# Attention order of a two-layer head-group mixer: half-width products gathered into three groups per head pair

## The reference, cut to what matters

```python
def block_attention(q, k, v, scale):           # 20 maps: 6 of gqa, 8 of diff, 6 of mla
    s = einsum('bqkgd,blkd->bkgql', q, k) * scale
    p = softmax(s, axis=-1)
    return einsum('bkgql,blkd->bqkgd', p, v)
# latent queries read context and latent keys (256 + 512); context queries read context keys only
o_a  = block_attention(ql_a, [kc_a, kl_a], [vc_a, vl_a], 64**-0.5)
o_b  = diff_out(block_attention(q1l, ...), block_attention(q2l, ...), lam, ...)   # o1 - lam*o2, rms norm
o_m  = block_attention(ql_m, [kc_m, kl_m], [vc_m, vl_m], 96**-0.5)
if ctx_out:                                     # layer 0 only
    oc_a, oc_b, oc_m = the same with context queries, context keys and values
h = concat([o_a * silu(g_a), o_b * silu(g_b), o_m * silu(g_c)])
y = h @ w_out
```

## Time and profile before

| | |
|---|---|
| runs before | 1100.06, 1102.35, 1105.29 us |
| the profiled execution | 1105.77 us, its span 1103.9 us |
| TensorE busy | 969.0 us (88%) |
| VectorE, ScalarE, GpSimd busy | 594.0, 403.4, 524.8 us |
| mean granted TensorE clock | 0.928 of full speed |
| TensorE's share of the chain that ended last | 71% |

### The profile page before, as it was taken

The page is one execution under the profiler, slowest core; times in us unless marked ns, Lnnn a source line. Parts: engine busy times, 40 slices in busy tenths (PEclk is TensorE's granted clock), DMA queues, the critical chain, the costliest instruction groups (busy, mean ns, idle before and its releaser), DMA issues.

```text
span 1103.9 us, 13093 instructions
## 1 busy us (share of the span) xinstructions
PE 969.0 (88%) x4607; PEld 684.6 (62%) x4607; DVE 594.0 (54%) x901; ACT 403.4 (37%) x815; POOL 524.8 (48%) x421
## 2 busy tenths in 40 slices
PE   4799999996899899998995299899968999999793
PEld 2478777985554455555784289789755445555572
DVE  5419230244568499824069548341645758782337
ACT  1521122314354466554200333133434445555320
POOL 2227232352557455553345337243626756566464
PEclk9799999996899899999998689899959989899997
DMA  9756451215232100012431022123142130001421
GB/s 364 270 178 218 157 188 40 77 31 125 55 77 65 34 16 8 16 58 79 169 96 77 38 62 72 58 65 85 49 101 65 37 72 16 15 16 58 160 69 77
DMA packets 44976, 96.91 MB, mean 88 GB/s; under 512 B 9592, under 2 KB 16656, under 8 KB 42864
## 3 DMA queue, kind: packets, MB, share of 16 engines
q1 hardware_dynamic: 43472, 90.83, 26.8%
q10 hardware_dynamic: 1440, 5.24, 1.2%
HBM read 71.33 MB, written 5.26 MB: 69 GB/s over the span
## 4 chain that ended last, share of the span: by engine, by line
PE 71%; DVE 10%; POOL 4%; ACT 4%; SPq 4%; DMA 3%; issue 3%; POOLq 0%; ACTq 0%; DVEq 0%
PE banks L762 13%; PE banks L764 12%; PE banks L763 12%; PE banks L936 11%; PE banks L956 9%; PE banks L914 5%; SPq L588 3%; PE banks L773 2%; DMA area_g<-in_w_ada_dram 2%; DVE negmax L1635 1%; PE banks L975 1%; DVE stats L1515 1%; DVE area_b L1779 1%; PE banks L968 1%; PE banks L826 1%
## 5 line engine op out<-in xcount | busy, mean ns | idle before, releaser
L1393 POOL TENSOR_TENSOR w_split<-w_raw,w_split 128x512 fp32r<-128x512 f32 (+4 forms) x124 | 146.2, 1184 | 258.7 <-ACT w_split L1138 258.6
L762 PE MATMUL banks<-w_split,area_a 128*128 128x512 f32 (+3 forms) x624 | 232.7, 373 | 16.4 <-DVE area_a L1845 9.9
L764 PE MATMUL banks<-w_split,area_a 128*128 128x512 f32 (+3 forms) x624 | 229.8, 368 | 0.0
L763 PE MATMUL banks<-w_split,area_a 128*128 128x512 f32 (+3 forms) x624 | 229.7, 368 | 0.0
L1635 DVE TENSOR_REDUCE negmax<-banks 128x1 f32<-128x768 f32 x160 | 149.6, 951 | 67.3 <-PE banks L914 66.4
L1138 ACT ACTIVATE w_split<-w_raw 128x512 fp32r<-128x512 f32 (+4 forms) x124 | 69.9, 581 | 278.1 <-PE banks L764 278.1
L936 PE MATMUL banks<-area_a 97*128 97x512 f32 (+4 forms) x448 | 135.7, 416 | 17.5 <-DMA area_a<-m_row 11.5
L762 PEld LDWEIGHTS banks<-w_split,area_a 128*128 128x128 f32 x624 | 119.4, 191 | 46.2 <-issue 16.4
L1237 ACT ACTIVATE area_z<-banks 128x512 f32<-128x512 f32 x196 | 109.1, 595 | 103.5 <-PE banks L936 98.2
L764 PEld LDWEIGHTS banks<-w_split,area_a 128*128 128x128 f32 x624 | 118.9, 190 | 16.6
L763 PEld LDWEIGHTS banks<-w_split,area_a 128*128 128x128 f32 x624 | 119.2, 191 | 15.5
(11 more groups left out here) (184 smaller groups left out, 1458.4 us busy)
## 6 DMA issues: line engine op xcount, KB each, us to landing
area_g<-in_w_ada_dram SPq DMA_DIRECT2D x16, 1024.0 KB, 5.8
w_raw<-in_w_in_dram SPq DMA_DIRECT2D x32, 512.0 KB, 3.7
area_g<-in_w_ada_dram SPq DMA_DIRECT2D x16, 512.0 KB, 5.0
w_raw<-in_w_out_dram SPq DMA_DIRECT2D x16, 512.0 KB, 3.9
area_a<-parts SPq DMA_DIRECT2D x72, 96.0 KB
area_a<-parts SPq DMA_DIRECT2D x30, 192.0 KB, 3.6
area_b<-in_x_dram SPq DMA_DIRECT2D x8, 512.0 KB, 9.8
x_mid<-area_b ACTq DMA_DIRECT2D x6, 512.0 KB, 2.7
```

Source lines behind the costliest of these rows:

```text
L762: nc.tensor.matmul(dst, a[0], b[0], start=first, stop=False)
L763: nc.tensor.matmul(dst, a[0], b[1], start=False, stop=False)
L764: return nc.tensor.matmul(dst, a[1], b[0], start=False, stop=last)
L1393: op = nc.gpsimd.tensor_tensor(lo, raw, hi.bitcast(F32), ALU.subtract)
```

## The change

Each `attend(L)` is rewritten around one loop over p = 0 to 10, in which pair p is scored while pair p-1 is finished:

- In layer 0 the context scores of a pair come first instead of last.
- The half-width products stand in three groups per step: `mix(p-1, 4)` and `mix(p-1, 5)`; then the context product, `mix(p, 0)`, `mix(p, 1)` and `denominators`; then `mix(p, 2)` and `mix(p, 3)`. The context denominators of pair p and the latent ones of pair p-1 share one call, so there is one more call (p = 0) in layer 0.
- How many maximum tiles stand between them is read from the table `max_counts`.
- `turn_max(p+1)` comes earlier in a step (except at p = 0).
- On ScalarE `mla_high(2p+6)` now follows the last exponent and `squares` at the end of step p; `mla_high(2p+5)` stands between the exponents of steps 2 and 3.
- On GpSimd the gate of pair p-1 comes before the fourth sum, block 10 is split after that sum, and a diff pair's gate comes a step later.
- The rows of ones of all diff units and of four mla units are written once per layer: eight transfers in a row after the maxima of pair 1 (`load_ones`). Units 12 and 13 are loaded in turn 4 instead of 3, unit 14 in 4 instead of 5, unit 16 in 5 instead of 6.
- Reciprocals are a step of their own; the copied context output has two buffers.

The diff, cut to this:

```diff
+def max_counts(L, p):
+
+    if L < DEPTH - 1:
+        return {0: [1, 2, 0, 1, 2, 1, 1, 1, 0, 1, 3], 1: [1, 1, 2, 2, 1, 1, 0, 1, 1, 1, 0]}.get(p, [1, 1, 1, 1, 1, 1, 0, 1, 1, 1, 0])
+    return {0: [1, 0, 1, 1, 2, 1, 1, 0, 1, 1, 2], 1: [2, 1, 1, 1, 1, 1, 0, 1, 1, 1, 0]}.get(p, [1, 0, 1, 1, 1, 1, 0, 1, 1, 1, 0])
+
+
 NRING = 3
...
-            def load_one(row, done):
-                move(row.rearrange("o (t n) -> o t n", n=P), across(ones_r[:], TILES)).then_inc(done, 16)
+            def load_ones():
+
+                for b in range(1, 2 * KD, 2):
+                    move(blocks[96:97, b, :].rearrange("o (t n) -> o t n", n=P), across(ones_r[:], TILES)).then_inc(ones_in, 16)
 
...
-                    for u in {-1: (2, 3), 0: (4, 5), 1: (6, 7), 2: (8, 9), 3: (10, 11, 12, 13), 5: (14, 15),
-                              6: (16, 17), 7: (18, 19)}.get(p, ()):
+                    for u in {-1: (2, 3), 0: (4, 5), 1: (6, 7), 2: (8, 9), 3: (10, 11), 4: (12, 13, 14), 5: (15, 16),
+                              6: (17,), 7: (18, 19)}.get(p, ()):
                         load_unit(L, u)
...
                 if L == 0:
                     pe.wait_ge(ada_ready, 2)
-                for i in range(len(max_tiles(L))):
-                    max_tile(L, 0, i)
+                tiles = iter([(p, i) for p in range(NPAIR) for i in range(len(max_tiles(L)))])
+
+                def maxima(n):
+                    for p, i in itertools.islice(tiles, n):
+                        max_tile(L, p, i)
+
+                maxima(len(max_tiles(L)))
                 turn_max(L, 0)
...
-                for p in range(1, NPAIR):
-                    scores(L, p, 0)
-                    max_tile(L, p + 1, 6)
-                    scores(L, p, 1)
-                    max_tile(L, p + 1, 7)
-                    if context:
-                        mix(L, p - 1, "ctx")
-                    else:
+                for p in range(NPAIR + 1):
+                    c = max_counts(L, p)
+                    now = p < NPAIR
+                    if now and context:
+                        scores(L, p, "ctx")
+                    maxima(c[0])
+                    if now:
+                        scores(L, p, 0)
+                    maxima(c[1])
+                    if p:
                         mix(L, p - 1, 4)
                         mix(L, p - 1, 5)
-                    scores(L, p, 2)
-                    max_tile(L, p + 1, 8)
-                    denominators(L, p - 1)
-                    scores(L, p, 3)
-                    max_tile(L, p + 2, 0)
-                    turn_denominators(L, p - 1)
-                    turn_output(L, p - 1)
-                    mix(L, p, 0)
-                    max_tile(L, p + 2, 1)
-                    turn_max(L, p + 1)
-                    mix(L, p, 1)
+                    maxima(c[2])
+                    if now:
+                        scores(L, p, 1)
+                    maxima(c[3])
+                    if now:
+                        if context:
+                            mix(L, p, "ctx")
+                        mix(L, p, 0)
+                        mix(L, p, 1)
+                    if p or context:
+                        denominators(L, p)
+                    if p:
+                        turn_max(L, p + 1)
+                    maxima(c[4])
+                    if now:
+                        scores(L, p, 2)
+                    maxima(c[5])
+                    if now:
+                        scores(L, p, 3)
+                    maxima(c[6])
                     if head_pair(p + 3):
                         mla_head(L, 2 * p + 6)
-                    scores(L, p, 4)
-                    max_tile(L, p + 2, 2)
-                    scores(L, p, 5)
-                    max_tile(L, p + 2, 3)
-                    mix(L, p, 2)
-                    max_tile(L, p + 2, 4)
+                    if now:
+                        mix(L, p, 2)
+                        mix(L, p, 3)
+                    if p or context:
+                        turn_denominators(L, p)
+                    maxima(c[7])
+                    if p:
+                        turn_output(L, p - 1)
+                    maxima(c[8])
+                    if now:
+                        scores(L, p, 4)
+                    maxima(c[9])
+                    if p == 0:
+                        turn_max(L, 1)
                     if head_pair(p + 3):
                         mla_head(L, 2 * p + 7)
-                    mix(L, p, 3)
-                    max_tile(L, p + 2, 5)
-                    if context:
-                        scores(L, p, "ctx")
-                        mix(L, p, 4)
-                        mix(L, p, 5)
-
-                if context:
-                    mix(L, NPAIR - 1, "ctx")
-                else:
-                    mix(L, NPAIR - 1, 4)
-                    mix(L, NPAIR - 1, 5)
-                denominators(L, NPAIR - 1)
-                turn_denominators(L, NPAIR - 1)
-                turn_output(L, NPAIR - 1)
+                    if now:
+                        scores(L, p, 5)
+                    maxima(c[10])
 
...
@@ -1285,50 +1293,47 @@
                 split_block(L, 2)
                 copy_maxrow(L, 0)
 
-                exponent(L, 0, 0)
-                exponent(L, 0, 1)
-                split_block(L, 4)
-                for s in range(2, 6):
-                    exponent(L, 0, s)
-                copy_maxrow(L, 1)
-                split_block(L, 6)
-                if context:
-                    exponent(L, 0, "ctx")
-
-                for p in range(1, NPAIR):
-                    exponent(L, p, 0)
-                    if context:
+                for p in range(NPAIR + 1):
+                    now = p < NPAIR
+                    if now and context:
+                        exponent(L, p, "ctx")
+                    if now:
+                        exponent(L, p, 0)
+                    if p:
                         copy_latents(L, p - 1)
-                    if head_pair(p + 2):
-                        mla_high(L, 2 * p + 4)
-                    exponent(L, p, 1)
-                    if context:
-                        copy_context(L, p - 1)
-                    else:
-                        copy_latents(L, p - 1)
+                    if now:
+                        exponent(L, p, 1)
+                    if p == 0:
+                        split_block(L, 4)
+                    if now and context:
+                        copy_context(L, p)
+                    if p or context:
+                        copy_denominators(L, p)
+                    if p:
+                        copy_maxrow(L, p + 1)
+                    if now:
+                        exponent(L, p, 2)
                     if head_pair(p + 2):
                         mla_high(L, 2 * p + 5)
-                    exponent(L, p, 2)
-                    copy_denominators(L, p - 1)
-                    exponent(L, p, 3)
-                    copy_maxrow(L, p + 1)
+                    if now:
+                        exponent(L, p, 3)
                     if head_pair(p + 3):
                         mla_copy(L, 2 * p + 6)
-                    exponent(L, p, 4)
-                    exponent(L, p, 5)
+                    if now:
+                        exponent(L, p, 4)
+                    if p == 0:
+                        copy_maxrow(L, 1)
+                        split_block(L, 6)
+                    if head_pair(p + 3):
+                        mla_copy(L, 2 * p + 7)
+                    if now:
+                        exponent(L, p, 5)
                     if (L, p - 1) in N_NORMED:
                         squares(L, p - 1)
-                    if head_pair(p + 3):
-                        mla_copy(L, 2 * p + 7)
                     if p == 2:
                         split_block(L, 10)
-                    if context:
-                        exponent(L, p, "ctx")
-
-                copy_latents(L, NPAIR - 1)
-                if context:
-                    copy_context(L, NPAIR - 1)
-                copy_denominators(L, NPAIR - 1)
+                    if head_pair(p + 3):
+                        mla_high(L, 2 * p + 6)
 
...
@@ -1464,27 +1469,24 @@
                     split_w(("uq", L, j, 0))
                 split_block(L, 2)
                 for p in range(NPAIR + 1):
-                    diff = (L, p - 1) in N_NORMED
-                    if p < NPAIR:
-                        sum_probs(L, p, 1)
+                    if (L, p - 2) in N_NORMED:
+                        gate(L, p - 2)
                     if p == 0:
                         split_block(L, 4)
                     if p < NPAIR:
+                        sum_probs(L, p, 1)
                         sum_probs(L, p, 2)
-                    if p and not diff:
+                        sum_probs(L, p, 3)
+                    if p and (L, p - 1) not in N_NORMED:
                         gate(L, p - 1)
-                    if p < NPAIR:
-                        sum_probs(L, p, 3)
```

(31 more changed lines are left out.)

201 lines of the change are left out of this document (85 added, 116 removed).

## The result

The changed kernel takes 1123.52 us (median of 4, 1122.08 to 1129.64), the kernel before 1101.2 us beside it (4 runs, 1099.5 to 1105.29): a ratio of 1.0208, 95% interval 1.0160 to 1.0256. It is slower, and my 1101 us with its range up to 1117 missed it. The profiled executions, 1123.4 and 1105.77 us with spans of 1121.5 and 1103.9, differ by 17.6 us in their spans.

The account below looks back on a forecast made before the run. TensorE's queue was taken as the bound. Edges -19.4, added work +1.4, idle -21.7, small delays -3, half clock -11, new waits +40.8 and their half clock +12 gave -0.9, hence 1101 us; 8-in-10 range 1083 to 1117.

Parts of the forecast that it names:

- Edges, -19.4: TensorE, both attentions: 61 fewer runs of half-width products at 0.35 us, less 2.0 for denominators, save 19.4 us.
- Rival 3: TensorE's groups: gathering saves no edges, as 0.35 us belongs to the first product of each kind; 1118 us, chance 0.08.
- The 14.4 us: Alternative edge saving by the skill's rule: 64 to 32 columns also changes mode, so only 41 groups save.
- smaller spacings: Small delays between scores, not shown as idle, go: 3 us over twenty steps, 0.15 each.
- Idle time, -21.7 + 40.8: TensorE, both attentions: all old idle time but the tail's 0.8 us goes, 21.7; new waits bring 40.8 us.
- behind squares and mla_high, steps 5 to 7: Layer 0, second unit of scores 0 waits for ScalarE's queue: 3.1, 3.1 and 2.3, together 8.5 us.
- behind the split of block 10: Unit 10's transfers come late for its first maximum tile: 5.3 us in layer 0, 3.8 in layer 1, sum 9.1.
- the other "small ones": Small waits in each step besides the output's bank: scores outrunning exponents, mixes 1 and 2, pair 1's maxima row; 8.8 us.
- VectorE, 1 us: New waits because VectorE is full in layer 1's mla steps: 1 us.
- Half clock, -11 + 12: Half clock after old waits goes, 11 us; new waits of 5.3, 3.8 and half of those near 3 us bring 12.
- Rival 2: ScalarE's queue at pair starts, layer 0 steps 5 to 7: 3.1 us waits bring half clock, VectorE late; 1112 us, chance 0.20.
- Rival 1: New waits are covered: they come at two thirds, with half clock for only two; 1082 us, chance 0.25.

Follow-up runs that it names:

- a14: a10 with a maximum tile of layer 0 put between the context mix and mix 0, 68 runs of half-width products instead of 60; 1092.24 us, 0.9902.
- b1: Kernel before with only mixes grouped (maximum tile and turn moved, mixes 2 and 3 together), 91 runs of half-width products instead of 121; 1103.93 us, 1.0003.
- b4: Kernel before with b1's groups, the change's table of loads, and one gain in each of steps 1 to 4 instead of four in step 2; 1088.85 us, 0.9882.
- a3: Changed kernel with maximum tiles put back between mixes 4 and 5 and mixes 2 and 3, 85 runs of half-width products instead of 60; 1150.9 us, 1.0431.
- b5: b4 with the rows of ones written once, behind units 6 and 7, and waited for by the scores alone; 1088.23 us, 0.9853.
- a13: a10 with a maximum tile put between mix 1 and the denominators, 75 runs of half-width products instead of 60; 1101.31 us, 0.9983.
- a10: a9 with, in layer 0 from step 4, pair p+2's first maximum tile behind the denominators and mla_low ahead of the last sums; 1092.25 us, 0.9909.
- a9: Changed kernel with squares before second mla copies, mla_high behind next exponents 0, block 10 split early, gains spread, ones behind units 6 and 7; 1109.16 us, 1.0053.
- a12: Changed kernel with only the two edits that a10 adds to a9 (first maximum tile later, mla_low earlier); 1121.96 us, 1.0180.
- a1: Changed kernel with mla_high of the next pair's second unit moved from a step's end to behind the next pair's exponents 0; 1125.56 us, 1.0205.

## Why the prediction was wrong

**Edges, -19.4.** The price was right where nothing hides it: 0.33 to 0.34 us in three steps of a14, 0.35 forecast, and 0.20 for denominators, where I had 0.25. Sums over whole kernels give 0.34 (b1), 0.26 (b4), 0.25 (a3) and 0.23 (b5) for mixes, 0.26 for contexts and 0.21 for denominators. By the highest of these the 61 runs are 30 x 0.34, 11 of contexts at 0.26 and 20 of denominators at 0.21: 17.3 us; with 0.23 for mixes they are 14.0. Rival 3 is refuted by b1 and by the steps of a14. The 14.4 us that I worked out by the Trainium skill (TensorEngine Tiling (Array Packing), Tiling Modes, Key Properties) took the denominators' edge as lost; the trace of a13 doesn't bear that out. It doesn't contradict the rule either. A run of denominators split off makes three changes of width where there were two, and a run of mixes split off makes two for 0.34, or 0.17 each; 0.20 is near that. No run tells this reading from mine.

With pair 0's denominators and smaller spacings I had -21; measured is -10.7. Of these 10.3 us the prices are 2.1, or up to 5.4 by the lowest sums. The rest, 8.2 to 5, are the spacings: I had 3 us less of them, and there are some 2 to 5 us more, waits of a quarter of a microsecond inside products, as scores 1 of a10 show. They are idle time in no view. That they make up the whole rest is inferred.

**Idle time, -21.7 + 40.8.** It went from 22.5 to 40.7 us in the windows as the earlier trace rows cuts them, where I had 41.6. The sum is right, the parts partly by luck:

| | forecast | measured |
|---|---|---|
| behind squares and mla_high, steps 5 to 7 | 8.5 | 7.0 |
| behind the split of block 10 | 9.1 | 8.2 |
| behind rows of ones | 2.2 | 2.9 |
| behind gains | 4.2 | 2.2 |
| mla_high ahead of exponents 3 | 1.8 | 0.45 |
| output's bank | 3.2 in "small ones" | 3.1 |
| the other "small ones" | 8.8 | 0.3 |
| VectorE, both layers | 1 | 10.0 |
| ScalarE's split ahead of context exponents, step 3 | 0 | 1.35 |
| tail | 2 | 2.8 |

The term that failed here is **VectorE, 1 us**. I had "full in layer 1's mla steps" and charged it nothing in layer 0, where the table of maxima asks for a pair's first tile before mla_low has made its operands. Of the 10.0 us, 2.2 are that tile (1.43 and 0.77); its real weight is larger, since ScalarE's waits stand ahead of it, as a9 and a10 show. 5.2 are late reductions from step 3 of layer 1 on, nearly all in its mla steps (1.38, 1.38 and 1.77 the longest), the mechanism that I named and priced at 1. 2.6 are waits in the first steps of both layers, which the kernel before has too and which I had counted as gone. That the sum came out right is luck: VectorE's 9 us too little met 8.5 us of small waits that didn't show as idle. Those are probably the ones hidden in products.

**Half clock, -11 + 12.** This term failed most: +7.8 for my +1. I gave half clock to the two long waits and to half of those near 3 us. It followed nine: 4.78, 3.40, 2.76, 2.75, and also 1.93, 1.51, 1.38 (twice) and 1.35 us. I had reasoned from the earlier trace rows, where 2.47 us brought none and 2.50 did, as if a wait's length decided. By all executions on record the term is off by more: half clock rose by 13 us.

**Outside attention, 0**: +2.1, of which 1.8 behind layer 1's attention, where half clock is 10.0 us for 7.9, without a cause in the change that I can show. Stretches with identical work differ as much between executions: the 280 us ahead of attention held between 15 and 20 us of half clock in these kernels.

**Rival 2** had the place and the direction (a wait of 3.1 us in each of steps 5 to 7 whose half clock counts, VectorE late behind it), and priced the end at 1112. Its point of decision was met: these waits did bring half clock. It deserved more than 0.20. What it lacked is that VectorE is a cause of its own, as a9 and a10 show. **Rival 1** is refuted for the large waits (7.0 of 8.5 us and 8.2 of 9.1 came); of the small ones most didn't show as idle, and it didn't help.

So of the 18.5 us by which the sum missed the span, 10.3 are work, 6.8 half clock and 2.1 lie outside, less 0.7 of idle time forecast too high. Settled is that the loss lies in the queues and not in the groups or in context first: a10 keeps both and is 0.9% faster than before. But it isn't faster than b4 and b5, which keep the old order with half of the runs saved; that the other 31 runs bring anything, no run shows. What stays open is which of the small waits inside products belong to which queue; no view names them. Nor was the way from a9 to a10 taken apart: its two edits ran only together. Nor does a run tell why half clock followed these waits and not others.

## What to carry to other kernels

When a new order moves a consumer, walk every producer of its operands to it, not only the engine that is idle today: here ScalarE's copies held the second scores of a pair and VectorE's remainders a maximum tile a few microseconds behind them, and mending one showed nothing. Take the cheap part of such a change alone first; groups, loads and gains in the old order gave -1.2% with no new queue. And charge each new wait above a microsecond with a chance of half clock. Where it comes, it can cost as much again (2.75 us of it behind a wait of 2.75); over all waits it was 7.8 us on 18.4 of new idle time in this pair of executions. Compare kernels by several executions and their granted clocks, since one profile of each can hide this.

## What the runs showed of the hardware

- The granted clock after a wait doesn't follow from the wait's length. In the changed kernel 1.51 us at 463.01 was followed by 0.57 over 4 us; in a12 the same wait of 1.52 at 463.59 by 1.00, and in both the 4 us ahead of the wait were at full clock. In a1 1.30 us was followed by 0.58 and 1.72 by 1.00. In a9 a wait of 1.52 us at 458.21 was followed by 1.00 and one of 1.52 at 928.64 by 0.57.
- A run of 64-column products between 128-column ones costs 0.33 to 0.34 us where nothing hides it (steps 4, 7 and 8 of a14 against a10), about 0.1 of it at the product and the rest at the next ones. Fusing 32-column products to 64-column ones saves 0.20; the denominators themselves take 0.99 us in a group (a10, step 7) and 1.00 alone (a13).
- An order that makes 10 us less work can have the same time within 0.3% (b1): TensorE arrives earlier at the same late tile and waits 3.89 us for 2.47, and half clock follows.
- The kernel before, unchanged, lost between 68 and 88 us of its 1100 to half clock from one execution to the next (span times one less the mean granted clock, 59 executions).
